# One transformer kernel, two edits: the last projection with tokens on partitions, and attention work issued in joined runs

## The chip, the cores and the metric

The kernel runs on one core of one Trainium2 chip. The metric is the device time of one execution in microseconds (us); lower is better. Three runs of the kernel before gave 1349.24, 1351.93 and 1356.86 us, median 1351.93. A profiled execution is one further run, with every instruction recorded.

## The reference

One sequence of 256 tokens with 1024 features passes through two blocks, all in float32. The first block has a modulated feed-forward net, a mixer that adds a short convolution and an attention of 8 query and 2 key heads, and a second feed-forward net. The second block has an even layer (gated recurrent heads and stick-breaking attention) and an odd layer (pooling). What the change touches:

```python
# first block: q and k are normed per head of 128 features, rotated, and attend
q = rms_norm(q.reshape(B, L, 8, 128), q_g);  k = rms_norm(k.reshape(B, L, 2, 128), k_g)
q = apply_axial_rope(q, cos, sin);           k = apply_axial_rope(k, cos, sin)
p = softmax(q @ k.T * 128 ** -0.5);          o = p @ v
# second block, mLSTM of the even layer: gates per head, broadcast over features
# second block, end of the odd layer, which is the kernel's output
y = (mixed * silu(z)) @ w_out            # 256 x 2048 @ 2048 x 1024
out = x + y * rsqrt(mean(y * y, axis=-1) + 1e-6) * post_g
```

## The kernel before

Activations lie with features on partitions and tokens along the free axis: `X[:, k, 256:512]` holds features 128k to 128k+127 of all 256 tokens. Each large product is made of three: weights and activations are split into a high and a low part in a rounded float32 format (`WH`, `WL`, `XH`, `XL` and so on), and TensorE adds high x high, high x low and low x high (lines 1038 to 1040; 1044 to 1046 where tokens are to lie on partitions, as for the values of the attention). Weights arrive in chunks of 4 x 128 rows by 256 columns: SyncE loads them (`W`), ScalarE makes the high part (`WH`, line 1458), VectorE the low part (`WL`, line 1863). A chunk is 24 products.

The order of all engines comes from one list, written by the class `Plan`. It walks through the large products; after each half chunk (12 products) it calls `tick`, which lets one of the background generators (`qk_norm`, `attention`, `mlstm`, ...) put its next step into the list. A `yield` in a generator is thus one half chunk of distance. Every engine then goes through the list and emits its own part of each step, so what is early in the list is early in the queue of every engine. Background steps take their PSUM tiles from banks 4 to 6 in turn (`bank`), the large products use banks 0 to 3, sums for norms bank 7 (`NB`).

Names that the change and the steps touch:
- `qk_norm`: the step `qs` squares a head on ScalarE, `qa` sums over its features by a matmul with 4 columns (`hot`, line 1125), `qb` broadcasts the reciprocal roots of a group of four heads from 4 rows to 128 partitions (line 1131), `rope` rotates by a matmul with `perm` (line 1136).
- `attention`: 16 rounds. `score` is one matmul of 512 columns (line 1142), a maximum and a scale on VectorE (lines 2045, 2047) and the exponential on ScalarE (line 1550). `scale` divides by the sum on VectorE (lines 2052, 2054), `turn` transposes four 128x128 blocks (line 1147) and ScalarE copies them out, `gather` multiplies by the values (line 1154), every second round.
- `m0` of `mlstm`: two broadcasts of gates from 4 rows (lines 1182, 1183), then the score products (lines 1189, 1191).
- evictions on VectorE in the mixer: `vc` (convolution, lines 1755 to 1764, eight small instructions a product), `bg`, `mc`.
- the end: products `p1` (four, of 16 x 128 rows and 256 columns), sums of squares by GpSimd and three matmuls with ones (`ones`, line 1000), the step `post` with the root on ScalarE (line 1525), the reciprocal (line 2010) and for each of eight feature tiles a multiply and an add on VectorE (lines 1718, 1724), and a DMA for each tile (line 979).
- GpSimd otherwise does nothing but the sums of squares (line 1256).

## Time and profile before

| what | value |
|---|---|
| median of three runs | 1351.93 us |
| profiled execution: its time, its span | 1357.65 us, 1355.9 us |
| mean granted TensorE clock | 0.989 of full speed |
| TensorE matmul busy | 1320.6 us, 97% |
| VectorE busy | 906.0 us, 67% |
| ScalarE busy | 648.1 us, 48% |
| GpSimd busy | 30.3 us, 2% |
| chain that ended last | TensorE 88%, VectorE 7%, ScalarE 3% |

The span runs from the first to the last instruction. Busy shares do not add up, since the engines work beside one another. The chain that ended last is followed back from the last instruction through whatever released each step. Matmuls are pipelined: one of 256 columns is recorded with about 0.28 us, but the next starts 0.11 to 0.12 us after it, so prices are read from starts. A matmul in full float32 appears as two records.

### The profile page before, as it was taken

What the parts mean: (1) busy time and instruction counts of PE and PEld (TensorE: products, weight loads), DVE (VectorE), ACT (ScalarE), POOL (GpSimd) and SP (SyncE); (2) the same over time, 40 slices, a digit from 0 to 9 for tenths busy, and PEclk for the clock granted to TensorE, in tenths of its full rate; (3) what the DMA queues carried; (4) which work ended last, traced back from release to release, by engine and by line L of the source; (5) the groups of instructions that cost most, each with busy time, mean ns of one, the idle gap of its engine ahead of it and who ended that gap; (6) DMA issues with size and microseconds to landing.
All of it is one profiled execution on the core that took longest, in us unless ns stands there. A gap on an engine that the chain in (4) does not pass through costs nothing.

```text
span 1355.9 us, 23439 instructions
## 1 busy us (share of the span) xinstructions
PE 1320.6 (97%) x9310; PEld 1212.0 (89%) x9310; DVE 906.0 (67%) x1462; ACT 648.1 (48%) x1025; POOL 30.3 (2%) x29
## 2 busy tenths in 40 slices
PE   6999999999999999999999999999999999999996
PEld 3688888888898889999999999998999999999996
DVE  3577875646658487654775555678886665689873
ACT  4433222223236335554454444566665765556552
POOL 0000000000010000000000000200000000100000
PEclk6999999999999999999999999999999999999998
DMA  8755656465544334444546655565546455437650
GB/s 303 262 166 188 206 193 218 161 216 184 176 153 156 109 113 152 127 150 148 183 142 186 199 175 172 155 188 157 169 135 193 126 166 177 140 119 215 196 172 32
DMA packets 201404, 229.69 MB, mean 169 GB/s; under 512 B 7120, under 2 KB 191696, under 8 KB 201296
## 3 DMA queue, kind: packets, MB, share of 16 engines
q1 hardware_dynamic: 201008, 227.90, 53.0%
q8 instruction: 75, 1.23, 0.4%
q14 instruction: 33, 0.27, 0.1%
q10 hardware_dynamic: 288, 0.29, 0.1%
HBM read 227.11 MB, written 1.05 MB: 168 GB/s over the span
## 4 chain that ended last, share of the span: by engine, by line
PE 88%; DVE 7%; ACT 3%; issue 2%; DMA 0%; DVEq 0%; ACTq 0%
PE P L1038 26%; PE P L1039 25%; PE P L1040 25%; DVE WL L1863 1%; PE P L1044 1%; PE P L1046 1%; PE P L1045 1%; PE P L1154 1%; DVE TS L1791 1%; PE P L1142 1%; PE P L1000 1%; PE P L1084 1%; DVE TS L1663 1%; ACT WH L1458 1%; PE P L1131 1%
## 5 line engine op out<-in xcount | busy, mean ns | idle before, releaser
L1038 PE MATMUL P<-XHB,WH 128*128 128x256 f32 (+1 forms) x1808 | 561.2, 310 | 7.5 <-DVE XLB L1675 3.7
L1039 PE MATMUL P<-XLB,WH 128*128 128x256 f32 (+1 forms) x1808 | 545.9, 302 | 0.0
L1040 PE MATMUL P<-XHB,WL 128*128 128x256 f32 (+1 forms) x1808 | 545.7, 302 | 0.0
L1863 DVE TENSOR_TENSOR WL<-W,WH 128x1024 fp32r<-128x1024 f32 x358 | 431.1, 1222 | 100.1 <-ACT WH L1458 99.9
L1458 ACT ACTIVATE WH<-W 128x1024 fp32r<-128x1024 f32 x358 | 368.7, 1041 | 251.4 <-PE P L1040 175.8
L1038 PEld LDWEIGHTS P<-XHB,WH 128*128 128x128 f32 x1808 | 341.9, 189 | 35.4 <-issue 14.0
L1039 PEld LDWEIGHTS P<-XLB,WH 128*128 128x128 f32 x1808 | 340.7, 188 | 18.0 <-issue 3.1
L1040 PEld LDWEIGHTS P<-XHB,WL 128*128 128x128 f32 x1808 | 340.6, 188 | 14.6
L1038 PE MATMUL P<-GH,WH 128*128 128x256 f32 (+1 forms) x372 | 122.0, 328 | 0.0
L1040 PE MATMUL P<-GH,WL 128*128 128x256 f32 (+1 forms) x372 | 121.5, 327 | 0.0
L1039 PE MATMUL P<-GL,WH 128*128 128x256 f32 (+1 forms) x372 | 121.5, 326 | 0.0
L1739 DVE TENSOR_TENSOR TS<-TS,P 128x512 f32<-128x512 f32 (+1 forms) x44 | 24.3, 554 | 83.0 <-PE P L1040 83.0
L1038 PEld LDWEIGHTS P<-GH,WH 128*128 128x128 f32 x372 | 70.7, 190 | 6.4 <-issue 0.2
L1039 PEld LDWEIGHTS P<-GL,WH 128*128 128x128 f32 x372 | 70.0, 188 | 6.4 <-issue 0.2
L1040 PEld LDWEIGHTS P<-GH,WL 128*128 128x128 f32 x372 | 70.0, 188 | 6.0
L1930 DVE CUSTOM_DVE_ANT_0 W<-W,AC,V 128x1024 f32<-128x1024 f32 x56 | 72.7, 1298 | 0.0
L1327 ACT ACTIVATE GH<-TS 128x512 fp32r<-128x512 f32 (+1 forms) x44 | 23.1, 526 | 92.3 <-DVE TS L1739 92.3
L1321 ACT ACTIVATE TS<-P 128x512 f32<-128x512 f32 (+1 forms) x44 | 21.4, 491 | 86.5 <-PE P L1040 86.5
L1256 POOL TENSOR_TENSOR SQ<-SQ 128x256 f32<-128x256 f32 (+1 forms) x25 | 30.1, 1205 | 1303.8 <-ACT SQ L1282 1302.7
L1749 DVE SCALAR_TENSOR_TENSOR X<-P,GM,X 128x256 f32<-128x256 f32 x48 | 21.5, 480 | 53.5 <-PE P L1040 53.4
L1044 PE MATMUL P<-WH,XHB 128*128 128x256 f32 x160 | 45.6, 285 | 1.1 <-DVE WL L1863 1.0
L1046 PE MATMUL P<-WH,XLB 128*128 128x256 f32 x160 | 44.5, 278 | 0.0
(302 smaller groups left out, 1813.8 us busy)
## 6 DMA issues: line engine op xcount, KB each, us to landing
W<-in_ffn_w_in SPq DMA_DIRECT2D x88, 512.0 KB, 4.8
W<-in_w_in_ab SPq DMA_DIRECT2D x72, 512.0 KB, 4.5
W<-in_w_modt SPq DMA_DIRECT2D x56, 512.0 KB, 3.9
W<-in_w_in SPq DMA_DIRECT2D x52, 512.0 KB, 3.6
W<-in_ffn_w_out SPq DMA_DIRECT2D x40, 512.0 KB, 4.6
W<-in_w_in_c SPq DMA_DIRECT2D x32, 512.0 KB, 4.3
W<-in_w_mod SPq DMA_DIRECT2D x16, 512.0 KB, 7.1
W<-in_w_out_ab SPq DMA_DIRECT2D x16, 512.0 KB, 4.4
```

The source lines that it names most:

```text
L1038: pe.matmul(o, h[:, k, c], xh[:, kk, a:b], start=kk == 0, stop=False)
L1039: pe.matmul(o, h[:, k, c], xl[:, kk, a:b], start=False, stop=False)
L1040: mm = pe.matmul(o, l[:, k, c], xh[:, kk, a:b], start=False, stop=kk == gm.nk - 1)
L1044: pe.matmul(o, xh[:, kk, c], h[:, k, :], start=kk == 0, stop=False)
L1046: mm = pe.matmul(o, xl[:, kk, c], h[:, k, :], start=False, stop=kk == gm.nk - 1)
L1256: pool.tensor_tensor(SQ[:, 0, 0:n], SQ[:, 0, 0:n], SQ[:, 1 + (k - 1) % 2, 0:n], ALU.add) \
L1327: act.activation(GH[m][:, f % 12, :], TS[:, f % NS, 0:n], ACT.Copy).then_inc(S[f"hh{m}"], 1)
L1458: act.activation(h, a, ACT.Copy).then_inc(S["wh"], 1)
L1739: dve.tensor_tensor(TS[:, f % NS, 0:n], TS[:, f % NS, 0:n], ps, ALU.mult).then_inc(S[f"hm{m}"], 1)
L1749: up = dve.scalar_tensor_tensor(X[:, k, ca:cb], ps[:, ca - a:cb - a], GM[:, m - 1, v, k:k + 1], X[:, k, ca:cb], ALU.mult, ALU.add)
L1863: dve.tensor_tensor(l, a, h.bitcast(F32), ALU.subtract).then_inc(S["wl"], 1)
L1930: td = dve.tensor_tensor_reduce(a if v == s.c - 1 else JK[:, :, :], a, (AC0, AC1)[v][:, :, :], 1.0, vec("bmod", 8 * g + k), ALU.mult, ALU. ...
```

## The change

It has two parts. The last projection `p1` gets its operands the other way round, so that tokens lie on partitions. Sums of squares then run along rows: ScalarE adds them up while it squares, one root per partition is taken from 128x1 numbers, the gain `pg` is loaded as a row for all partitions, the residual `X` is turned by 16 transposes behind the last product (step `xt`), and each half of the tokens is finished by two combines and two DMAs. In the attention, the score of the next round, the gather and the transpose come in one visit of the generator, the exponential becomes a step of its own behind them (`exp`), and the rotations of `qk_norm` share a visit with a broadcast. Along with that, the broadcasts of roots and gates and the head sums use all 128 rows and columns, the rest being zeros that GpSimd fills in (`HOT`, and two rows of tiles of `G`). The shape of `out_x` becomes tokens by features.

```diff
-        self.call(self.stats, "s7")
         for i in range(4):
-            self.gemm("p1", i, w["w_out_c_2"], 0, 16, 256 * i, (0, T), first=i == 0, norm=i == 3)
-        self.call(self.post, 1)
+            self.gemm("p1", i, w["w_out_c_2"], 0, 16, 256 * i, (0, T), turned=False, first=i == 0, norm=i == 3)
+        for i in range(4):
+            self.call(self.residual, i)
...
+    def residual(self, i):
+
+        self.step("xt", a=i, bank=4 + i, free=self.bank_free.get(4 + i, ("sr", self.roots["n", 5])))
...
             yield
         todo = None
         for i in range(4):
+            if todo is not None:
+                self.rope(*todo)
+                todo = None
             b, f = self.bank(self.up("qn"))
             self.step("qb", a=s, b=i, c=self.at("qn"), bank=b, free=f)
-            at = self.at("qn")
-            yield
-            if todo is not None:
-                self.rope(*todo)
-                yield
-                todo = None
             if s < 2 or i % 2:
-                todo = (s, i, at)
+                todo = (s, i, self.at("qn"))
             else:
                 self.ready.add(self.name(s, i))
-                self.end[self.name(s, i)] = at
+                self.end[self.name(s, i)] = self.at("qn")
+            yield
+            yield
         if todo is not None:
             self.rope(*todo)
 
...
         for _ in range(3):
             yield
         score(0)
+        self.step("exp", a=0, bank=4 + (self.uses - 1) % 3)
         for i in range(16):
-            yield
-            yield
+            for _ in range(2):
+                yield
             self.step("scale", a=i)
+            for _ in range(2):
+                yield
             if i + 1 < 16:
                 while missing(i + 1):
                     yield True
                 score(i + 1)
-            yield
+                bank = 4 + (self.uses - 1) % 3
             if i and i % 2 == 0:
                 b, f = self.bank(self.up("ol"))
                 self.step("gather", a=i // 2 - 1, bank=b, free=f)
-            yield
             b, f = self.bank(self.up("at"))
             self.step("turn", a=i, bank=b, free=f)
-        for _ in range(3):
+            if i + 1 < 16:
+                self.step("exp", a=i + 1, bank=bank)
+        for _ in range(2):
             yield
         b, f = self.bank(self.up("ol"))
         self.step("gather", a=7, bank=b, free=f)
...
+        HOT = MC[:, 0, 0:131]
-            G = sbuf(st, "G", [4, 6, T])
+            G = sbuf(st, "G", [128, 6, T])
-            return MC[0:4, 7, :] if s == 2 else RS[0:4, 1, T * s:T * s + T]
+            return MC[:, 7, :] if s == 2 else RS[:, 1, T * s:T * s + T]
...
+                if i == len(plan.loads) - 16:
+                    sp.wait_ge(S["k2p"], 8)
+                    sp.dma_start(PG, w["pg"].partition_broadcast(128).rearrange("p o c -> p (o c)")).then_inc(SI[5], 16)
...
-            for k in range(8):
-                sp.wait_ge(S["pst"], 8 + k + 1)
-                sp.dma_start(out[k * 128:k * 128 + 128, :], X[:, k, 256:512]).then_inc(S["out"], 16)
-            sp.wait_ge(S["out"], 16 * 8)
+            for n in range(4):
+                j, a = n // 2, n % 2
+                sp.wait_ge(S["p1o"], 4 * j + a + 3)
+                sp.dma_start(out[128 * j:128 * j + 128, 512 * a:512 * a + 512].rearrange("p (i c) -> p i c", i=2),
+                             X[:, 4 * j + 2 * a:4 * j + 2 * a + 2, 0:T]).then_inc(S["out"], 16)
+            sp.wait_ge(S["out"], 16 * 4)
...
-                    ones("s5" if s.a == 0 else "s7", 2)
-                    if s.a == 0:
-                        warm(3, s.b)
-                        pe.wait_ge(S["sr"], plan.roots["post", 0])
-                        warm(7, s.b)
+                    ones("s5", 2)
+                    warm(3, s.b)
+                    pe.wait_ge(S["sr"], plan.roots["post", 0])
+                    warm(7, s.b)
+                elif s.kind == "xt":
+                    pe.wait_ge(S["pst"], 8)
+                    for c in range(4):
+                        k = 4 * (s.a % 2) + c
+                        a = 256 + 128 * (s.a // 2)
+                        mm = pe.transpose(ps[:, c * 128:c * 128 + 128], X[:, k, a:a + 128], con("id"))
+                    mm.then_inc(S["xt"], 1)
                 elif s.kind == "qa":
+                    pe.wait_ge(S["fill"], 2)
                     for i in range(4):
                         n = 4 * s.a + i
                         pe.wait_ge(S["qs"], n + 1)
-                        pe.matmul(ps[0:4, 0:T], con("hot", 4 * i, 4 * i + 4), SQ[:, n % 3, T * (n // 3 % 2):T * (n // 3 % 2) + T], start=i == 0,
+                        pe.matmul(ps[:, 0:T], HOT[:, 3 - i:131 - i], SQ[:, n % 3, T * (n // 3 % 2):T * (n // 3 % 2) + T], start=i == 0,
                                   stop=i == 3).then_inc(S["qh"], 1)
                 elif s.kind == "qb":
                     pe.wait_ge(SI[5], 16)
                     if s.b == 0:
                         pe.wait_ge(S["qi"], s.a + 1)
-                    pe.matmul(ps[:, 0:T], con("sel", 128 * s.b, 128 * s.b + 128, 4),
+                    pe.matmul(ps[:, 0:T], con("sel", 128 * s.b, 128 * s.b + 128),
                               rows_of(s.a), start=True, stop=True).then_inc(S["qb"], 1)
...
-                    pe.matmul(ps[:, 0:T], con("sel", 128 * h, 128 * h + 128, 4), G[:, 4, 0:T], start=True, stop=True)
-                    pe.matmul(ps[:, T:2 * T], con("sel", 128 * h, 128 * h + 128, 4), G[:, 5, 0:T], start=True,
+                    pe.matmul(ps[:, 0:T], con("sel", 128 * h, 128 * h + 128), G[:, 4, 0:T], start=True, stop=True)
+                    pe.matmul(ps[:, T:2 * T], con("sel", 128 * h, 128 * h + 128), G[:, 5, 0:T], start=True,
...
+            pool.wait_ge(S["md"], 56)
+            pool.memset(HOT, 0.0).then_inc(S["fill"], 1)
+            pool.wait_ge(S["fill"], 1)
+            pool.memset(HOT[:, 3:4], 1.0).then_inc(S["fill"], 1)
...
+                if name == "s3":
+                    pool.wait_ge(S["oh"], 8)
+                    pool.memset(G[:, 4:6, :], 0.0).then_inc(S["fill"], 1)
...
-                        if kind == "p1":
-                            act.wait_ge(S["pst"], k + 1)
-                        act.activation(X[:, k, 0:T], ps, ACT.Copy, scale=vec("post" + kind[1], k)) \
-                            .then_inc(S[kind + "e"], 1)
+                            root_table(4)
+                        square("s5", k, (ps, 1.0))
+                        act.activation(X[:, k, 0:T], ps, ACT.Copy, scale=vec("post0", k)).then_inc(S["p0e"], 1)
+                    elif kind == "p1":
+                        if k == 4:
+                            root_table(5)
+                        if k >= 6:
+                            act.wait_ge(S["p1q"], k - 5)
+                        act.activation(SQ[:, k % 3, T * (k // 3 % 2):T * (k // 3 % 2) + T], ps, ACT.Square,
+                                       accum_out=FS[:, j, i:i + 1]).then_inc(S["p1q"], 1)
+                        if i == 3:
+                            act.wait_ge(S["p1o"], 4 * j + 1)
+                            act.activation(FS[:, j, 5:6], FS[:, j, 4:5], ACT.Sqrt, scale=1.0 / D, bias=con("eps")) \
+                                .then_inc(S["p1r"], 1)
...
-                elif s.kind == "score":
+                elif s.kind == "exp":
                     i = s.a
-                    act.wait_ge(S["am2"], i + 1)
+                    act.wait_ge(S["am1"], 2 * i + 2)
...
+            def root(j):
+
+                dve.tensor_reduce(FS[:, j, 4:5], FS[:, j, 0:4], AX, ALU.add).then_inc(S["p1o"], 1)
+                dve.wait_ge(S["p1r"], j + 1)
+                dve.reciprocal(FS[:, j, 6:7], FS[:, j, 5:6]).then_inc(S["p1o"], 1)
+                dve.wait_ge(S["p1o"], 4 * j + 2)
+                dve.wait_ge(S["p1e"], 6 + j + 1)
+                for a in range(2):
+                    y = X[:, 4 * j + 2 * a:4 * j + 2 * a + 2, 0:T]
+                    dve.wait_ge(S["xt"], 2 * j + a + 1)
+                    dve.scalar_tensor_tensor(y, y, FS[:, j, 6:7], P[:, 4 + 2 * j + a, :].rearrange("p (i c) -> p i c", i=2),
+                                             ALU.mult, ALU.add).then_inc(S["p1o"], 1)
...
+                        dve.wait_ge(S["p1q"], k + 1)
+                        dve.wait_ge(SI[5], 32)
+                        dve.tensor_tensor(X[:, 4 * j + i, 0:T], ps, PG[:, 256 * i:256 * i + 256], ALU.mult).then_inc(S["p1e"], 1)
+                        if i == 3:
+                            root(j)
...
-                    if s.a:
-                        for k in range(8):
-                            add(1, k)
...
-    out = nc.dram_tensor("out_x", (D, T), F32, kind="ExternalOutput").ap()
+    out = nc.dram_tensor("out_x", (T, D), F32, kind="ExternalOutput").ap()
     build_program(nc, aps, out)
     r = _run(nc, [{f"in_{n}": a for n, a in arrays.items()}], core_ids=[0])
-    return np.ascontiguousarray(r.results[0]["out_x"].T)[None]
+    return r.results[0]["out_x"][None]
```

The first place is TensorE's queue in the attention, in a round with a gather. `K,Q` is the score, `PT,VV` the gather, `C,TS` the transpose, `XHB,WH` and the like are large products. Before:

```order
L1040 MATMUL P<-XHB,WL 128x256
L1142 MATMUL P<-K,Q 128x512
L1038 MATMUL P<-XHB,WH 128x256
...
L1154 MATMUL P<-PT,VV 128x256 x4
L1038 MATMUL P<-XHB,WH 128x256
...
L1147 MATMUL P<-C,TS 128x128 x4
```

After:

```order
L1050 MATMUL P<-XHB,WL 128x256
L1159 MATMUL P<-K,Q 128x512
L1171 MATMUL P<-PT,VV 128x256 x4
L1164 MATMUL P<-C,TS 128x128 x4
L1048 MATMUL P<-XHB,WH 128x256
```

Three visits, 12 products apart, have become one. From a score to the transpose of the same round there are now 4 half chunks, before there were 6.

The second place is VectorE's queue in the same stage, from the maximum of a round (`TENSOR_REDUCE SM`) to its multiply (`TENSOR_SCALAR TS`), around the convolution of `vc3`. Before, the maximum comes behind the convolution or long ahead of it; in the round whose multiply waits for the convolution stands this:

```order
L1755 TENSOR_TENSOR U<-U,P 128x256
L1757 TENSOR_SCALAR TS<-U,V 128x256
L1760 SCALAR_TENSOR_TENSOR TS<-U,V,TS 128x256
L1764 SCALAR_TENSOR_TENSOR TS<-U,V,TS 128x256
L1863 TENSOR_TENSOR WL<-W,WH 128x1024
L2052 RECIPROCAL SM<-SM 128x1
L2054 TENSOR_SCALAR TS<-TS,SM 128x512
L2045 TENSOR_REDUCE SM<-P 128x1
L2047 TENSOR_SCALAR SM<-SM 128x1
```

After:

```order
L2090 TENSOR_REDUCE SM<-P 128x1
L2092 TENSOR_SCALAR SM<-SM 128x1
L1797 TENSOR_TENSOR U<-U,P 128x256
L1799 TENSOR_SCALAR TS<-U,V 128x256
L1802 SCALAR_TENSOR_TENSOR TS<-U,V,TS 128x256
L1806 SCALAR_TENSOR_TENSOR TS<-U,V,TS 128x256
...
L1911 TENSOR_TENSOR WL<-W,WH 128x1024
L2097 RECIPROCAL SM<-SM 128x1
L2099 TENSOR_SCALAR TS<-TS,SM 128x512
```

The maximum now stands directly ahead of the convolution (whose four instructions come twice), and the multiply of the same round behind it.

The third place is the end of VectorE's queue. Before, the last norm and the residual for each of eight tiles:

```order
L1718 TENSOR_TENSOR X<-X,RS 128x256
L1724 TENSOR_TENSOR X<-X 128x256
L1718 TENSOR_TENSOR X<-X,RS 128x256
L1724 TENSOR_TENSOR X<-X 128x256
```

After, from the last product with the gain of the first half of the tokens on:

```order
L1872 TENSOR_TENSOR X<-P,AC 128x256
L1757 TENSOR_REDUCE FS<-FS 128x1
L1759 RECIPROCAL FS<-FS 128x1
L1765 SCALAR_TENSOR_TENSOR X<-X,FS,P 128x2x256 x2
L1872 TENSOR_TENSOR X<-P,AC 128x256
L1757 TENSOR_REDUCE FS<-FS 128x1
L1759 RECIPROCAL FS<-FS 128x1
L1765 SCALAR_TENSOR_TENSOR X<-X,FS,P 128x2x256 x2
```

Sixteen instructions behind a reciprocal over 128x256 have become ten, with the combines of the first half ahead of the second half's gain.

## Rows read from the trace of the kernel before

**Rows 1.** The page: busy us and share of TensorE, records.

```profile
PE 1320.6 (97%) x9310; PEld 1212.0 (89%) x9310; DVE 906.0 (67%) x1462; ACT 648.1 (48%) x1025; POOL 30.3 (2%) x29
```

**Rows 2.** Waits of TensorE, one row: total us, times, longest us.

```profile
PE P L1147 <- DVE TS L2054: 0.5, 1, 0.5
```

**Rows 3.** Timeline of TensorE, a rotation: start us, duration us, instruction.

```profile
460.83 0.59 PE L1136 MATMUL P<-Q,C 128*128 128x256 f32 x2
...
461.38 0.28 PE L1039 MATMUL P<-XLB,WH 128*128 128x256 f32 x1
```

**Rows 4.** Timeline of TensorE, a broadcast of roots from 4 rows.

```profile
457.07 0.28 PE L1046 MATMUL P<-WH,XLB 128*128 128x256 f32 x1
457.28 0.69 PE L1131 MATMUL P<-RS,C 4*128 4x256 f32 x2
...
458.13 0.28 PE L1045 MATMUL P<-WL,XHB 128*128 128x256 f32 x1
```

**Rows 5.** Windows: stretch, length, busy us and records of each engine, clock, DMA.

```profile
699.00:880.00 181.00, 181.00 (x1538) 181.00 (x1538) 106.56 (x133) 92.19 (x132) 7.27 (x5) 1.00 0.59 181
...
1218.00:1341.00 123.00, 123.00 (x1085) 123.00 (x1086) 92.91 (x171) 68.83 (x113) 4.11 (x5) 1.00 0.53 163
```

**Rows 6.** Timeline of all engines, the tail behind the last product.

```profile
1343.50 0.28 PE L1040 MATMUL P<-RH,WL 128*128 128x256 f32 x1
...
1343.82 0.38 ACT L1282 ACTIVATE SQ<-P 128x256 f32<-128x256 f32 x1 [1.07 <-PE P L1040]
...
1345.49 1.75 DVE L2010 RECIPROCAL RS<-RS 128x256 f32<-128x256 f32 x1 [13.36 <-ACT RS L1525]
...
1353.30 0.43 DVE L1724 TENSOR_TENSOR X<-X 128x256 f32<-128x256 f32 x1
```

**Rows 7.** Timeline of TensorE, four transposes of the attention.

```profile
526.75 0.60 PE L1147 MATMUL P<-C,TS 128*128 128x128 f32 x4
...
527.30 0.28 PE L1039 MATMUL P<-XLB,WH 128*128 128x256 f32 x1
```

**Rows 8.** Groups by line: busy us, mean ns; the last, one line's durations.

```profile
L1739 DVE TENSOR_TENSOR TS<-TS,P 128x512 f32<-128x512 f32 x22 | 15.0, 687 | 54.7 <-PE P L1040 54.7
L2045 DVE TENSOR_REDUCE SM<-P 128x1 f32<-128x512 f32 x16 | 11.0, 687 | 4.9 <-PE P L1142 4.9
L2052 DVE RECIPROCAL SM<-SM 128x1 f32<-128x1 f32 x16 | 2.5, 156 | 0.0
L1288 ACT ACTIVATE SC<-C x5: 203/203/203, 389.7 to 1332.2; 128x1 f32<-128x1 f32 x5
```

**Rows 9.** DMA issues: count, KB each, median us from issue to landing.

```profile
W<-in_ffn_w_out SPq DMA_DIRECT2D x8, 256.0 KB, 4.3
out_x<-X SPq DMA_DIRECT2D x8, 128.0 KB, 1.7
```

**Rows 10.** Timeline of TensorE, a head sum with 4 columns, and four full matmuls.

```profile
475.80 1.89 PE L1125 MATMUL P<-SQ,C 128*4 128x256 f32 x8
...
477.85 0.28 PE L1039 MATMUL P<-XLB,WH 128*128 128x256 f32 x1
...
523.60 1.89 PE L1154 MATMUL P<-PT,VV 128*128 128x256 f32 x8
...
525.44 0.28 PE L1039 MATMUL P<-XLB,WH 128*128 128x256 f32 x1
```

**Rows 11.** Timeline of TensorE, the gates of one mLSTM head.

```profile
963.32 0.28 PE L1040 MATMUL P<-XHB,WL 128*128 128x256 f32 x1
...
966.12 0.28 PE L1045 MATMUL P<-WL,XHB 128*128 128x256 f32 x1
```

**Rows 12.** Timeline of VectorE, from a convolution's eviction to the multiply behind it.

```profile
544.21 0.42 DVE L1755 TENSOR_TENSOR U<-U,P 128x256 f32<-128x256 f32 x1 [1.26 <-PE P L1040]
...
549.08 0.49 DVE L2054 TENSOR_SCALAR TS<-TS,SM 128x512 f32<-128x512 f32 x1
```

**Rows 13.** One line of VectorE: durations, first and last start.

```profile
L1930 DVE CUSTOM_DVE_ANT_0 W<-W,AC,V x56: 1272/1279/2330, 72.2 to 368.8; 128x1024 f32<-128x1024 f32 x56
```

**Rows 14.** Timeline of GpSimd, the second sum of squares.

```profile
376.63 3.52 POOL L1256 TENSOR_TENSOR SQ<-SQ 128x512 f32<-128x512 f32 x2 [10.59 <-ACT SQ L1282]
```

More of the change, by code:

```diff
@@ L36 @@
 _at = 0
-for _name, _n in (("id", 128), ("one", 128), ("eps", 1), ("ee", 1), ("hot", 16), ("gat", 2), ("cnt", 26), ("perm", 128),
+for _name, _n in (("id", 128), ("one", 128), ("eps", 1), ("ee", 1), ("gat", 2), ("cnt", 26), ("perm", 128),
                   ("tri", 128), ("m01", 128), ("nst", 128), ("nca", 128), ("sel", 512), ("cos", 256), ("sin", 256)):
@@ L78, in constants @@
     put("ee", np.full((128, 1), EPS * EPS, np.float32))
-    hot = np.zeros((128, 4, 4), np.float32)
-    for i in range(4):
-        hot[:, i, i] = 1.0
-    put("hot", hot.reshape(128, 16))
     put("gat", (p[:, None] % 32 == np.arange(2)[None, :]).astype(np.float32))
@@ L846, in build_program @@
         seq, stat, end = plan.seq, plan.stat, plan.end
-        names = ("g wh wl zero sc mm mr mt mv md cb sf sq pa on sr ra ri rb am gm out sil1 hm1 hh1 hl1 xu1 sil2 hm2 hh2 hl2 xu2 "
+        names = ("g wh wl zero fill sc mm mr mt mv md cb sf sq pa on sr ra ri rb am gm out sil1 hm1 hh1 hl1 xu1 sil2 hm2 hh2 hl2 xu2 "
                  "nt nh nl xh xr rx "
                  "qe ke ve cge vce bge yh yl gte mce gae mae ma2 o2h o2l rse yc qs qh qr qi qb qn rm ro rd "
-                 "as am1 am2 ae an ap atp at agp oh ol two tw fr fin gr0 gmm gfree gab gq att cve cvs cvt cvq eve eoe "
-                 "ezt eze sqe ske sve szt sze m1 m1p m1t m2 m2p m3 m3p m4 m4p md1 md2 mhh m5 m5s m5p m5r m6 zh zl "
-                 "k1 k1p k1a k1l k1m k2 k2p k2e k3 k3p p0e p1e pst pm ope opc ph pl oze ome rh rl dv")
+                 "as am1 ae an ap atp at agp oh ol two tw fr fin gr0 gmm gfree gab gq att cve cvs cvt cvq eve eoe "
+                 "ezt eze sqe ske sve szt sze m1 m1p m1t m2 m2p m3 m3p m4 m4p md1 mhh m5 m5s m5p m5r m6 zh zl "
+                 "k1 k1p k1a k1l k1m k2 k2p k2e k3 k3p p0e p1e p1q p1r p1o xt pst pm ope opc ph pl oze ome rh rl dv")
         S = {n: ctx.enter_context(nc.semaphore(f"s_{n}")) for n in names.split()}
         SW = [ctx.enter_context(nc.semaphore(f"s_w{i}")) for i in range(WR)]
-        SI = [ctx.enter_context(nc.semaphore(f"s_in{i}")) for i in range(7)]
+        SI = [ctx.enter_context(nc.semaphore(f"s_in{i}")) for i in range(6)]
         def sbuf(st, name, shape, dt=F32):
@@ L877, in build_program @@
         RT = AM[:, 2, 1, 0:4]
+        FS = sbuf(ctx, "FS", [128, 2, 8])
         AC0 = sbuf(ctx, "AC0", [128, 4, 256])
@@ L2069, in _ @@
                     dve.wait_ge(S["gmm"], 1)
-                    dve.tensor_scalar(G[:, 1, 0:T], ps[0:4, T:2 * T], V[0:4, VEC["bf"][0]:VEC["bf"][1]], None, ALU.add) \
+                    dve.tensor_scalar(G[0:4, 1, 0:T], ps[0:4, T:2 * T], V[0:4, VEC["bf"][0]:VEC["bf"][1]], None, ALU.add) \
                         .then_inc(S["gfree"], 1)
                 elif s.kind == "g2":
-                    ig, b, t2, top, neg = (G[:, i, 0:T] for i in range(5))
+                    ig, b, t2, top, neg = (G[0:4, i, 0:T] for i in range(5))
                     dve.wait_ge(S["gfree"], 1)
@@ L2087, in _ @@
                     dve.wait_ge(S["dv"], own)
+                    dve.wait_ge(S["fill"], 3)
                     dve.tensor_scalar(neg, top, -1.0, None, ALU.mult).then_inc(S["dv"], 1)
```

59 lines of the change are left out of this document (28 added, 31 removed).

## The prediction

> **What bounds the kernel now.** I read the page first: TensorE is busy for 97% of the span [rows 1], on one core, and no other engine comes near it. The table of waits, limited to TensorE, then says how little it waits: in the stages that this change touches there is one entry that matters, a transpose of the attention that waited 0.5 us for VectorE [rows 2]. So time can come from three places only: from what TensorE issues, from the pace at which it issues, and from the tail behind the last product, where it has nothing left to do.
>
> *What it issues.* The timeline of TensorE shows an almost even stream of split products, one matmul of 256 columns each 0.11 to 0.12 us, broken by detours: small f32 matmuls for norms, attention and gates. The price of a detour is the time from the start of the product before it to the start of the second product behind it, less two ordinary steps. For a rotation by `perm` (128 rows, 256 columns) it is 461.38 - 460.83 - 0.12 = 0.43 us [rows 3]. For the broadcast of the roots, of the same 256 columns but with only 4 rows in the stationary and the moving operand, it is 458.13 - 457.07 - 0.24 = 0.82 us [rows 4]: the array stands for 0.1 us before it and for about 0.3 us behind it. Twelve such broadcasts are in the trace (24 records, two for an f32 matmul).
>
> *The pace.* The windows show that the even stream has two speeds although the granted clock is 1.00 (2.4 GHz) in all of them: 181.00 us / 1538 = 117.7 ns in the second feed-forward net, 123.00 / 1085 = 113.4 ns in the last stage [rows 5]. It changes only at a detour or a wait and then stays. Nothing in the diff aims at it, but it matters for the forecast below.
>
> *The tail.* From the start of the last product (1343.50) to the end of the span (1355.9) pass 12.4 us [rows 6]: the third sum by ones, the root over 128x256, a reciprocal of 1.75 us, eight times multiply and add on VectorE, and the last of eight DMAs.
>
> **The change, part by part.**
>
> *The tail.* Before, 3 matmuls with ones serve the last norm; the first of them stands inside the stream and costs a plain detour of 0.43 us, which goes. The new tail, from the start S of the last product:
> - TensorE turns the residual: 16 transposes, 4 to a bank. Four such transposes cost the attention 527.30 - 526.75 - 0.12 = 0.43 us [rows 7], so the first bank is ready at about S + 0.75 (the first answer to a product's end comes 0.32 us after its start, 1343.82 against 1343.50 [rows 6]), the second at S + 1.2, the last at S + 2.1.
> - The first half of the tokens is ahead: its last product ended 12 matmuls (1.4 us) earlier, so its square, sum, root and reciprocal are over by S + 0.7. VectorE's combine of 128x512 from PSUM is bounded by a 128x512 tensor op from PSUM, 0.69 us [rows 8]; with a scalar I take 0.70. Two of them end at S + 2.15.
> - Behind them on VectorE: the product with the gain for the second half (0.42), a sum over 4 numbers (0.16, as the reciprocal of 128x1 [rows 8]), on ScalarE a root of 128x1 (0.20 [rows 8]), the reciprocal (0.16), two combines (1.40), and four hand-overs of about 0.03: S + 4.6.
> - The last DMA. Now 2.17 us pass from the end of the last add (1353.30 + 0.43) to 1355.9, for 128 KB that landed in 1.7. The new piece is 256 KB. A 256 KB load took 4.3 us among others, 1.7 is for half the size [rows 9]. These are the two ends; the nearest row is the quiet 1.7, so I take 2.7 in all, at S + 7.3.
> The tail shrinks from 12.4 to 7.3, and with the detour the part is worth 5.1 + 0.4 = **5.5 us** (between 3.5 with a 4.3 us landing and 6.5).
>
> *The order of operands in the last product.* 384 products of 256 columns before and after; the values of the attention are made in the new order already, and such a product takes the same time. 0.
>
> *Full rows in the detours.* Twelve broadcasts go from 4 to 128 rows: 12 x (0.82 - 0.43) = **4.7 us**. Three column sums for q and k have 4 columns in the stationary operand: 477.85 - 475.80 - 0.12 = 1.93 plus 0.1 of entry = 2.03 us, where four full matmuls of the same width take 525.44 - 523.60 - 0.12 = 1.72 [rows 10]: 3 x 0.31 = **0.9 us**. The gates of the mLSTM begin with two 4-row broadcasts: 966.12 - 963.32 - 0.23 = 2.57 us for 1280 columns [rows 11], where full matmuls take 0.43 per 256, so 2.15; 3 x 0.42 = **1.3 us** (the first of the four heads keeps its 4-row transposes and so its switches). The other bound of all three is 0: the trace has no padded form of these very operations.
>
> The Trainium skill speaks on both sides here. "TensorE: Matmul & The Clock Gate", section "LDWEIGHTS (loading the stationary operand)", says that the row count does not matter, a 32-row load takes as long as a 128-row one; by that the padding would be worth nothing and the whole change 5.5 us. "TensorEngine Tiling", Key Properties, says that changing the tiling mode drains the engine; by that each 4-row detour pays twice, and padding removes it. The two detours of [rows 3, 4] differ by 0.39 us, so the trace sides with the second page.
>
> *The joined runs of the attention.* Score, gather and transpose stood apart, each between products; now they follow one another. A plain full-row detour costs no more than its own columns (0.43 for 256 [rows 3]), so joining saves at most some 0.01 us each, 0.3 in all. Against that, a score now has 4 half chunks (4 x 1.36 us) until its transpose, before 6. In series behind the score (512 columns, so 0.86 us) lie the maximum, 0.69 [rows 8], a scale, the copy of the previous transpose and the exponential on ScalarE over 512 columns each, a reciprocal and a multiply; six steps of at most 0.7 us with the score are about 4 us, which fits. But twice (`vc2`, `vc3`) VectorE must first evict a convolution: from its first instruction to the multiply pass 549.08 - 544.21 = 4.9 us, the queue that made the wait of [rows 2, 12]. Started after the maximum, 1.95 us behind the score's start, it ends at 6.85 + 0.49 = 7.3, and the transpose is due at 0.86 + 0.44 + 5.44 = 6.7: two waits of about 0.5 us. The old one (0.5, with its gap 0.67) goes. I book **0** (between -1 and +2).
>
> *Fills by GpSimd.* The first fill waits for the 56th modulation row (last at 368.8 [rows 13]) and stands ahead of the sums of squares. They need it only by 376.63, where the second sum began [rows 14]: about 6 us of slack. The load of the gain sits in SyncE's queue behind a wait for a sum that is over some 130 us earlier, and the queue runs ahead. 0; without that slack it would delay a norm by 1 to 2 us.
>
> Sum: 5.5 + 4.7 + 0.9 + 1.3 = 12.4 us. The profiled execution took 1357.65 (span 1355.9), so it would be 1345.3. It is the slowest of the four known times, 5.7 above the median of the runs, 1351.93; the slow pace in the second feed-forward net alone is 181 us x (1 - 113.4/117.7) = 6.6 us, about that distance, so I take the sum from the median: 1351.93 - 12.4 = **1339.5 us**. Its own range is 1334 to 1345.
>
> **Rivals.**
> 1. *The pace decides.* The runs lie at 1349 to 1357 with one program. A changed row of detours draws anew in which stretches the slow pace holds: one net more or less is 6.6 us, so 1333 or 1346. For it: the two paces and the spread. Against: a median of several runs evens it out.
> 2. *Full rows gain nothing*, because the 0.39 us comes from something else that a root broadcast does: 1339.5 + 6.9 = 1346.4. Against: three different operations show an excess, and the full-row forms between them do not.
> 3. *The attention becomes bound by its own chain (slower).* Place: the transposes, which wait for the multiply on VectorE. The price is what VectorE's queue adds per round; at 0.5 us in all 15 rounds the time is 1347. It decides from (12.4 + 6.8) / 15 = 1.3 us a round on, and with a whole eviction and a split in series in each round (2 us) the time is 1339.5 + 30 = 1369. For it: VectorE is the one engine with a full queue there. Against: only the convolution evictions are long, and they end with `vc3`.
> 4. *The new tail keeps its length*, the landing taking 4.3 us and the transposes coming late: 1339.5 + 3 = 1342.5.
>
> **How the numbers follow.** Forecast 0.66, rival 1 0.14 (half of it on each side), rival 2 0.06, rival 3 0.08 (0.04 mild at 1347, 0.04 slower), rival 4 0.06. Half a percent of 1351.93 is 6.8 us, about what a measurement of this kernel can tell from no change, so faster means below 1345.2 and slower above 1358.7. Faster: 0.66 x 0.96 + 0.07 + 0.06 = 0.76, and some of rivals 1 and 2 falls just below: 0.80. Slower: 0.04. The rest, 0.16, is same. Range: 1332 to 1348; it takes in rivals 1, 2, 4 and the mild form of 3.
>
> **What would show it.** The padded broadcasts in the timeline at 0.43 us by the count above; the sums at 1.72; the gates at 2.15. From the last product's start to the end 7 to 8 us; no reciprocal over 128x256 behind it. At most two or three waits of the transposes for VectorE, all below 1 us. Wrong would be: a gap ahead of and behind the padded forms as before, a table of waits in which the attention's transposes stand with 5 us or more, or a step of the stream that differs over whole stages from that of before.

## The result, and the profile after

| | before | after |
|---|---|---|
| median of 20 runs | 1357.17 us (1349.24 to 1363.64) | 1348.61 us (1347.10 to 1351.25) |
| ratio, 95% interval | | 0.9945, 0.9930 to 0.9961 |
| profiled execution: time, span | 1357.65, 1355.9 | 1351.25, 1349.3 |
| start of the last product to the end | 12.4 us | 7.3 us |

The change is faster by about 7.4 us, where 12.4 were forecast. The time itself, 1348.61, lies just outside the range of 1332 to 1348. The forecast started from 1351.93, the median of the first three runs of before; the median of all 20 is 5.2 us higher. These medians need one remark: its runs fall into two groups, 1349 to 1353 and 1355 to 1364, in shares that differ from one set of rounds to the next (5 of 20 here in the lower group, 30 of 31 in another set). The experiments show what such groups can come from. So a difference between two kernels is worth most where single stages are compared, and ratios carry their intervals.

I read the profile after by the steps of the prediction. The page first: TensorE has the span to itself as before [rows 1].

```profile
PE 1318.4 (98%) x9320; PEld 1219.2 (90%) x9320; DVE 903.8 (67%) x1461; ACT 645.1 (48%) x1026; POOL 27.0 (2%) x27
```

*The detours.* The timeline of TensorE (start, duration, instruction) at one broadcast of roots, which answers to [rows 4], then at one head sum, for [rows 10], and at the gates, for [rows 11]:

```profile
457.24 0.28 PE L1056 MATMUL P<-WH,XLB 128*128 128x256 f32 x1
457.36 0.59 PE L1148 MATMUL P<-RS,C 128*128 128x256 f32 x2
...
457.91 0.28 PE L1055 MATMUL P<-WL,XHB 128*128 128x256 f32 x1
...
474.21 0.28 PE L1050 MATMUL P<-XHB,WL 128*128 128x256 f32 x1
474.33 1.89 PE L1142 MATMUL P<-SQ,MC 128*128 128x256 f32 x8
...
476.17 0.28 PE L1049 MATMUL P<-XLB,WH 128*128 128x256 f32 x1
...
958.52 0.28 PE L1050 MATMUL P<-XHB,WL 128*128 128x256 f32 x1
...
960.93 0.28 PE L1055 MATMUL P<-WL,XHB 128*128 128x256 f32 x1
```

The broadcast costs 457.91 - 457.24 - 0.23 = 0.44 us, where 0.43 was forecast and 0.82 stood before; the gap ahead of it is gone (0.12 from the product before, a plain step). The sum costs 476.17 - 474.21 - 0.24 = 1.72 (forecast 1.72), the gates 960.93 - 958.52 - 0.23 = 2.18 (forecast 2.15). These three terms came out to a tenth of a microsecond.

*The tail.* The timeline of all engines behind the last product, for [rows 6]:

```profile
1341.99 0.28 PE L1056 MATMUL P<-WH,RL 128*128 128x256 f32 x1
...
1342.11 1.91 PE L1135 MATMUL P<-C,X 128*128 128x128 f32 x16
...
1342.85 1.41 DVE L1765 SCALAR_TENSOR_TENSOR X<-X,FS,P 128x512 f32<-128x512 f32 x2 [0.45 <-PE P L1135]
1343.62 3.39 SPq L988 DMA_DIRECT2D out_x<-X  x4
...
1345.21 1.41 DVE L1765 SCALAR_TENSOR_TENSOR X<-X,FS,P 128x512 f32<-128x512 f32 x2
```

The first combine starts 0.86 us behind the last product (its bank was forecast ready at 0.75), the last ends at 1345.21 + 1.41 = 1346.62, S + 4.63 (forecast 4.6), and 2.7 us pass from there to the end (forecast 2.7): 7.3 in all.

*The attention.* The table of waits of TensorE (total, times, longest) has no row for its transposes any more; the wait of [rows 2] has gone and the two that I expected did not come. The first rows:

```profile
PE P L1083 <- DVE SQ L1932: 7.3, 2, 4.4
PE P L1048 <- DVE XLB L1707: 3.7, 3, 1.4
PE P L1087 <- DVE TS L1939: 3.4, 1, 3.4
```

*Where the time is lost.* Detours and tail give what was forecast, and yet the last product starts at 1341.99 where it started at 1343.50: 1.5 us earlier, not 7.3. What is left is the pace of the stream, told below in ns a step, where a step is the time from the start of one product to the start of the next. The last projection, before and after:

```profile
1299.97 0.28 PE L1038 MATMUL P<-RH,WH 128*128 128x256 f32 x1
1300.09 0.28 PE L1039 MATMUL P<-RL,WH 128*128 128x256 f32 x1
1300.20 0.28 PE L1040 MATMUL P<-RH,WL 128*128 128x256 f32 x1
1300.31 0.28 PE L1038 MATMUL P<-RH,WH 128*128 128x256 f32 x1
```

```profile
1299.99 0.28 PE L1054 MATMUL P<-WH,RH 128*128 128x256 f32 x1
1300.11 0.28 PE L1055 MATMUL P<-WL,RH 128*128 128x256 f32 x1
1300.23 0.28 PE L1056 MATMUL P<-WH,RL 128*128 128x256 f32 x1
1300.35 0.28 PE L1054 MATMUL P<-WH,RH 128*128 128x256 f32 x1
```

Three steps took 0.34 us and take 0.36. By starts over long stretches the paces before were 113.3 and 117.8 ns a step; now there is a third, 120.0, at a granted clock of 1.00 as before. I took the starts of all groups of three products, stage by stage, and summed what they spend above 113.33 ns a step: 18.7 us in the trace before, 24.2 in the one after. The 5.5 us between them are what is missing: 5.1 (tail) + 0.4 + 6.7 (detours) + 0.8 (waits of the attention) - 5.5 = 7.5, and the spans differ by 6.6. Most of the 0.9 left lies in the first 40 us: the first matmul with `ROW` behind the first large products starts at 38.18 where it started at 37.39. The same products ran longer at the lower of the two clocks (1.2 GHz, a granted clock of 0.5) before TensorE was given 2.4 GHz. Over the stretch from 34 to 38 us the granted clock (third number from the end) was 0.89 before and 0.63 after:

```profile
34.00:38.00 4.00, 3.50 (x29) 2.21 (x27) 0.40 (x1) 0.38 (x1) 0.00 (x0) 0.89 0.11 23
```

```profile
34.00:38.00 4.00, 3.67 (x22) 1.84 (x20) 0.13 (x1) 0.26 (x1) 0.00 (x0) 0.63 0.00 0
```

A second trace of the changed kernel (`a_again` below) has 0.85 there, so this is no doing of the change.

The third pace holds in the products with `YH`, `OH`, `GH`, `ZH`, `PH` and `RH` alone. Those with `XHB` between them stay at 113.3 or 117.8. That asks for what such a tensor is to TensorE: a place in SBUF. The sizes of the tensors, taken to lie one behind the other in order of allocation, give the places. The change takes `hot`, 16 numbers or 64 bytes per partition, out of the constants `C`, which moves `X`, `W`, `WH`, `WL`, `XHB`, `XLB` and all up to `SC` down by 64 bytes. Behind `SC` it puts `FS`, 64 bytes, so that the operands of the stages stay where they were. From `WH` to `RH` there were 102080 bytes, 192 more than a multiple of 256; now there are 102144, a multiple of 256. The other stage operands of 256 columns stand in the same way. The allocations have gaps named `PAD2` to `PAD7`, which no instruction reads or writes, and `XHB` and `XLB` are a little longer than their data, so that two views of them can start at different places: all of it sets such distances.

### The profile page after: what moved, and what is told of

The parts are those of the page before. It is cut to its first block and busy times, and to the rows that moved or that the text cites. A ratio compares the mean times of both kernels' runs of the same rounds, so it can differ in the third digit from the quotient of the medians.

```text
span 1349.3 us, 23450 instructions
## 1 busy us (share of the span) xinstructions
PE 1318.4 (98%) x9320; PEld 1219.2 (90%) x9320; DVE 903.8 (67%) x1461; ACT 645.1 (48%) x1026; POOL 27.0 (2%) x27
## 5 line engine op out<-in xcount | busy, mean ns | idle before, releaser
L1048 PE MATMUL P<-XHB,WH 128*128 128x256 f32 (+1 forms) x1808 | 554.1, 306 | 7.2 <-DVE XLB L1707 3.7
L1054 PE MATMUL P<-WH,XHB 128*128 128x256 f32 x160 | 45.7, 285 | 1.3 <-DVE WL L1911 1.0
L1055 PE MATMUL P<-WL,XHB 128*128 128x256 f32 x160 | 44.7, 279 | 0.0
```

Source lines behind the costliest of these rows:

```text
L1048: pe.matmul(o, h[:, k, c], xh[:, kk, a:b], start=kk == 0, stop=False)
L1054: pe.matmul(o, xh[:, kk, c], h[:, k, :], start=kk == 0, stop=False)
L1055: pe.matmul(o, xh[:, kk, c], l[:, k, :], start=False, stop=False)
```

## Experiments

Medians and ratios are to the kernel before in the same rounds. The theories: A, the distance between weight tiles and stage operands sets the pace; B, the pace is drawn anew by any change in the row of detours; C, the turned product is slower.

**The places put back** (`a_place`, and once more as `a_place2`), on the changed kernel: a gap of 16 numbers where `hot` was, and `FS` allocated behind `PV`, as the last of all:

```diff
-... ("ee", 1), ("gat", 2), ...
+... ("ee", 1), ("gap", 16), ("gat", 2), ...
-        FS = sbuf(ctx, "FS", [128, 2, 8])
+            FS = sbuf(st, "FS", [128, 2, 8])
```

> The changed kernel with the places of before in SBUF: the 64 bytes of the table hot stay as a gap among the constants, and FS is allocated last. No instruction changes. Theory A (place): the pace of the large products hangs on where the operands of a stage (YH, OH, GH, ZH, PH, RH) lie against the weight tiles (WH, WL); the change moved the latter by 64 bytes and the former not. Then these products come back from 120.0 ns a step to 118 or less, and the time falls by about the 5.5 us that the forecast missed: 1343 us where the changed kernel has 1348.6, ratio to before 0.991. Theory B (draw): the pace is drawn anew by any change in the row of detours, whatever the places: the ratio stays 0.9945 within 0.001 and the stage products stay at 120.0 ns.

> a_place once more. Expected 1336 to 1337 us. If the choice between 113.4 and 117.8 ns is made anew in each execution, the last stage, at 117.8 in the first profile, or the second feed-forward net, at 113.4 there, can stand at the other pace, and the time goes with it; if it belongs to the program, all stages have the paces of the first profile.

Measured: 1336.56 us, ratio 0.9882 (0.9854 to 0.9910), and 1336.23, 0.9864 (0.9823 to 0.9904). The gain is larger than A had it, since the 5.5 us were read against a trace of before whose second net ran at 117.8 ns. B, which had the ratio at 0.9945 and the stage products at 120.0 ns, fell here and falls again with `b_shift`.

**The changed kernel again**, in the rounds of `a_place2`:

> The changed kernel once more, on the same chip and in the same rounds as a_place2. If the 64 bytes explain what the forecast missed, it stands at 1348 to 1349 us, about 12 us above a_place2, and its stage products are at 119 to 120 ns again (YH, OH, GH, ZH, PH, RH), without any at 113.4. If the paces are drawn anew in each execution, some of them are at 113.4 or 117.8 now.

Measured: 1348.93 us, 0.9948 (0.9923 to 0.9973), 12.7 us above `a_place2`. One row shows the pace of 381 steps in each: the third product with `RL`, 128 times, with first and last start (line, durations, starts). In the changed kernel, `a_again`, `a_place` and `a_place2`:

```profile
L1056 PE MATMUL P<-WH,RL x128: 283/283/284, 1296.3 to 1342.0; 128*128 128x256 f32 x128
```

```profile
L1056 PE MATMUL P<-WH,RL x128: 282/283/284, 1294.5 to 1340.2; 128*128 128x256 f32 x128
```

```profile
L1056 PE MATMUL P<-WH,RL x128: 278/280/282, 1288.2 to 1333.1; 128*128 128x256 f32 x128
```

```profile
L1056 PE MATMUL P<-WH,RL x128: 275/276/280, 1283.2 to 1326.3; 128*128 128x256 f32 x128
```

45.7 us in both executions of the changed kernel, 45.7 / 381 = 119.9 ns. With the places of before 44.9 us (117.8 ns) in one execution and 43.1 (113.1) in the other. So there is a draw, and it is made in each execution of one and the same program: the profiled run of `a_place` took 1342.84 us, its other five 1334.82 to 1337.12, and the profiled run of `a_place2` 1335.41. But between these two sets of places the draw is between 113.3 and 117.8 and was seen at the places of before alone; at the shifted ones the pace is 120.0 in both traces.

**The shift alone** (`b_shift`), on the kernel before:

```diff
         SC = sbuf(ctx, "SC", [128, 16])
+        sbuf(ctx, "PADX", [128, 16])
```

> The kernel before with 64 unused bytes behind SC, so that AC0 and all stage operands lie 64 bytes further from the weight tiles, the same distance as in the changed kernel; no instruction changes. Theory A: the products with PH, RH and ZH go from 113.4 to 119 to 120 ns, those with OH, YH and GH from 117.8 to 120 ns: about 8 us more, less what XHB gains (up to 3), so a ratio of 1.003 to 1.006. Theory B: ratio 1.000 and 113.4 ns in the last stage as before.

Measured: 1361.74 us, ratio 1.0067 (1.0042 to 1.0092), where A had 1.003 to 1.006. 64 bytes that nothing reads cost 9 us. Here the weight tiles kept their places and the operands moved, in the change it was the other way round; the paces are the same in both, so it is the distance that counts and not either place. Against the 15 of before's 24 runs that lie below 1352 (median 1350.3) the price is 11.5 us. The products with `RH`, here the moving operand, went to the third pace too: 46.2 us with a detour of 0.43, (46.2 - 0.43) / 381 = 120.1 ns.

```profile
L1041 PE MATMUL P<-RH,WL x128: 281/283/284, 1301.4 to 1347.6; 128*128 128x256 f32 x128
```

**One stage alone** (`a_pad7`), on `a_place`:

```diff
-            sbuf(st, "PAD7", [128, 64])
+            sbuf(st, "PAD7", [128, 80])
```

> a_place with 64 bytes more ahead of RH and PH alone (the gap of the last stage 320 bytes long, not 256); all other operands stay. Place theory: only the products with PH and RH go to 119 to 120 ns, 576 products of which the 384 with RH cost 2.2 to 6.6 ns each and the 192 with PH as much: 1.3 to 3.8 us more than a_place2, ratio 0.990 to 0.991; the stages before keep 113.4 or 117.8. Against it: another stage changes too, or this one doesn't.

Measured: 1339.97 us (1339.51 to 1340.43), 0.9875 (0.9833 to 0.9916), 3.7 above `a_place2`. The operands of the last stage alone went slow, the stages ahead kept paces seen at these places before (117.8 with `OH`, 113.3 with `GH`). The row as above, and for `OH`, which did not move, in `a_pad7` and then in the changed kernel (22.3 against 22.7 us for 189 steps):

```profile
L1050 PE MATMUL P<-OH,WL x64: 281/281/282, 634.7 to 657.0; 128*128 128x256 f32 x64
...
L1056 PE MATMUL P<-WH,RL x128: 283/283/286, 1285.3 to 1331.1; 128*128 128x256 f32 x128
```

```profile
L1050 PE MATMUL P<-OH,WL x64: 280/283/287, 638.0 to 660.7; 128*128 128x256 f32 x64
```

This trace also shows that the pace goes with the operands of the single product, and with nothing else that moved. In the last stage 24 products with `PH` and 48 or 144 with `XHB`, whose distance to the weights is that of before, follow one another without a detour between them. The first of such groups:

```profile
1213.13 0.28 PE L1048 MATMUL P<-PH,WH 128*128 128x256 f32 x1
...
1215.99 0.29 PE L1048 MATMUL P<-XHB,WH 128*128 128x256 f32 x1
...
1221.45 0.28 PE L1048 MATMUL P<-PH,WH 128*128 128x256 f32 x1
```

With `PH` a step takes (1215.99 - 1213.13) / 24 = 119.2 ns, with `XHB` right behind it (1221.45 - 1215.99) / 48 = 113.8 ns, and so it goes on up to the last projection; in the trace before both take 113.3. So it is the distance between the two operands of a matmul, and not a distance between other tensors, such as those that ScalarE and VectorE write meanwhile.

**Other distances** (`a_s32`, `a_s128`, `a_s192`): `a_place` with 8, 32 or 48 unused numbers behind `SC`, for distances of 224, 64 and 128 past a multiple of 256.

> a_place with 32 unused bytes behind SC, so the stage operands lie 224 bytes past a multiple of 256 from the weight tiles, where a_place has 192 and the changed kernel has 0. If only a distance of 0 is slow, this is as a_place: stage products at 113.4 or 117.8 ns, ratio 0.988 to 0.990. If 64-byte places matter (whole lines of the memory), 224 shares its line with 192, the same. If it grows with nearness, 119 ns and 0.991 to 0.994.

> a_place with 128 unused bytes behind SC: distance 64 past a multiple of 256. If only 0 is slow: as a_place, 113.4 or 117.8 ns in the products with OH, YH, GH, ZH, PH and RH, 0.988 to 0.990. If any place but the old one is slow: 120.0 ns as in the changed kernel, 0.994.

> a_place with 192 unused bytes behind SC: distance 128, as far from 0 as it goes. If only 0 is slow: 113.4 or 117.8 ns, 0.988 to 0.990. If the draw between 113.4 and 117.8 hangs on the distance too, this one shows a single pace in all stage products, 0.986 where it is 113.4.

Measured: 1347.97 us, 0.9974 (0.9962 to 0.9986); 1349.70, 0.9979 (0.9964 to 0.9993); 1348.73, 0.9981 (0.9969 to 0.9992). "Only 0 is slow" fell, and so did the other forecasts: all three lose most of the gain. Nor is it one slow pace for all other places. From the starts in the traces, ns a step:

| distance | kernel | `OH` | `GH`, second net | `ZH` | `PH` | `RH` |
|---|---|---|---|---|---|---|
| 192 | before | 117.8 | 117.8 | 113.5 | 113.3 | 113.4 |
| 192 | `a_place` | 117.8 | 113.4 | 113.4 | 117.8 | 117.8 |
| 192 | `a_place2` | 117.8 | 113.4 | 113.5 | 113.3 | 113.3 |
| 0 | after | 120.0 | 120.0 | 119.9 | 119.4 | 120.0 |
| 0 | `a_again` | 120.0 | 119.9 | 120.0 | 119.3 | 120.0 |
| 0 | `b_shift` | 120.0 | 119.9 | 120.0 | 119.1 | 120.0 |
| 224 | `a_s32` | 118.3 | 118.3 | 118.3 | 118.2 | 116.7 |
| 64 | `a_s128` | 117.8 | 117.8 | 113.7 | 117.8 | 113.4 |
| 128 | `a_s192` | 120.0 | 118.7 | 118.6 | 118.9 | 118.6 |

(`ZH` from the last 48 to 82 groups of its stage, where no detour stands between. In the traces of before, `a_place` and `a_place2`, 82 and 46 steps with `ZH` ahead of them ran at 117.8.) Each distance has paces of its own. Not all of the loss is theirs: in `a_s128` the products with `XHB`, whose distance did not change, spent 12.2 us above 113.3 ns a step, against 6.1 in `a_place2`, most of it because its second net drew 117.8; its runs lie in two groups too, three at 1345.4 to 1345.7 and seven at 1349.4 to 1350.8. `GH` of the first net, in products of 512 columns, adds to it: it stood at distance 0, and its pace there is 113.3 ns for 256 columns; a shift by 64 bytes makes it 114.5, by 32, 128 or 192 bytes 116.7. So the best distance is not even the same for all shapes, and I have no rule for it.

**Mixed distances** (`a_mix`): `a_place` with `PAD6` and `PAD7` of 96 numbers, distance 64 for the last two stages.

> a_place with 128 bytes more ahead of the operands of the last two stages (ZH, PH, RH), whose distance 64 gave 113.4 ns with RH and 114 with ZH in a_s128, but 117.8 with PH. If the pace belongs to the place: RH at 113.4, ZH at 114, PH at 117.8, so between 2 us faster than a_place2 and 1 us slower. If it was the draw: any mixture, the time within 3 us of a_place2.

Measured: 1338.66 us (1338.56 to 1346.19), 0.9879 (0.9833 to 0.9924). `RH` had 113.4 and `PH` 117.8 as in `a_s128`, but `ZH` 117.7 where that kernel had 113.7, so there is a draw at distance 64 as well. No gain over `a_place`.

**The parts of the change, one by one**, each on the kernel before with all places kept. `b_rows` has the full rows and their fills, `b_tail` the last projection and its tail, `b_join` the generators of the attention and of `qk_norm`; their diffs are the hunks of the change, each with the few semaphores that the change merged, which no run tests alone.

> The kernel before with nothing but the full rows: broadcasts of roots and gates and head sums over 128 rows and columns, with the fills by GpSimd; places in SBUF as before. The detours should cost 0.43, 1.72 and 2.15 us in place of 0.82, 2.03 and 2.57: 6.9 us less, ratio 0.995. Theory A expects the pace of before beside it (0.995 within 0.0015); theory B allows anything from 0.990 to 1.000 with another pattern of paces.

> The kernel before with nothing but the new last projection and its tail (FS allocated last, places as before). 5.5 us less by the tail and its detour, ratio 0.996, where the products of p1 keep 113.4 ns. Theory A says that they keep 113.4 or 117.8 ns, since the places are those of before; theory C (operands): the turned product itself is slower, 120.0 ns with RH in the stationary place, which costs 384 x 6.6 ns = 2.5 us and makes the ratio 0.998.

> The kernel before with nothing but the joined runs: score, gather and transposes of the attention in one visit, the exponential as a step of its own, a rotation beside a broadcast; places as before. Forecast: between -1 and +2 us, ratio 1.000, with two waits of the transposes of about 0.5 us. The chain theory (VectorE late in every round) gives waits of 0.5 us in 15 rounds, 1.005. The third theory (fewer breaks of the stream, so less to lose at each) gives up to 3 us less, 0.998, seen as a lower mean step between 500 and 633 us.

| kernel | median | ratio, interval | forecast |
|---|---|---|---|
| `b_rows` | 1345.36 | 0.9963, 0.9940 to 0.9986 | -6.9 us, 0.995 |
| `b_tail` | 1345.56 | 0.9948, 0.9926 to 0.9970 | -5.5 us, 0.996 |
| `b_join` | 1347.92 | 0.9976, 0.9963 to 0.9989 | 0 |
| product of the three | | 0.9887 | |
| `a_place` | 1336.56 | 0.9882, 0.9854 to 0.9910 | |
| after | 1348.61 | 0.9945, 0.9930 to 0.9961 | -12.4 us, 0.991 |

The parts multiply to what the change gives with its places kept. The lower groups alone say the same without the draw: in the rounds of `b_rows`, `b_tail` and `a_place` the lower group of before has a median of 1350.3 us, six of ten runs of `b_rows` have 1344.7 (5.6 us less) and seven of ten of `b_tail` 1345.0 (5.2 less); with the 3.1 between the medians of `b_join` and of before in its rounds that makes 13.9, where `a_place` is 13.7 below. Theory C fell with `b_tail`: the turned products ran at the same pace as the old ones.

```profile
L1056 PE MATMUL P<-WH,RL x128: 275/277/282, 1290.5 to 1333.7; 128*128 128x256 f32 x128
```

43.2 / 381 = 113.4 ns, with `RH` in the stationary place at distance 192.

`b_join` gives 3 us that I had booked at nothing. Two rounds of the attention, from a score to the one after the next, take 583.92 - 568.43 = 15.49 us before and 576.03 - 560.80 = 15.23 with the joined runs, with the same instructions in them. First before, then `b_join`:

```profile
568.43 1.02 PE L1142 MATMUL P<-K,Q 128*128 128x512 f32 x2
...
583.92 1.02 PE L1142 MATMUL P<-K,Q 128*128 128x512 f32 x2
```

```profile
560.80 1.02 PE L1145 MATMUL P<-K,Q 128*128 128x512 f32 x2
...
576.03 1.02 PE L1145 MATMUL P<-K,Q 128*128 128x512 f32 x2
```

That is 2.1 us in 8 pairs of rounds, and 0.8 us of waits go as well. The detours themselves cost the same, apart (0.86 + 0.86 + 1.73 + 2 x 0.44 = 4.33 in two rounds) or joined (1.30 + 3.03). The difference is the pace between them: the products with `XHB` in these rounds had 116.6 ns before and 116.8 in `b_rows`, but 113.6 in `b_join` and 113.7 in `a_place2`. This is the third theory of the expectation. It holds in 12 of the 14 traces: from the first score to the last the products with `XHB` had 115.8 to 116.8 ns in the four kernels with the detours apart (before, `b_rows`, `b_tail`, `b_shift`) and 113.5 to 113.8 in eight traces with joined runs. But `a_s32` and `a_s128` have joined runs too and had 116.6 and 117.4 there. So a detour can leave the stream in either pace, and joining them does not by itself fix which. Why the quicker one held is open.

## Why the prediction was wrong

*The step that failed* is the sentence on the pace: "Nothing in the diff aims at it." Nothing aims at it, but two lines of the diff set it, the removal of `hot` from the constants and the new tile `FS`. I had read both lines and costed them at nothing, as storage. The term that is missing is +12 us: `a_place2` against `a_again` gives 12.7 in the same rounds, `b_shift` against the lower group of before 11.5. Step by step: 525 products with `GH` in the second net x 6.5 ns = 3.4 us, 384 with `RH` x 6.7 = 2.6, 372 with `ZH` x 4.8 = 1.8, 192 with `PH` x 6.0 = 1.2, 192 with `OH` x 2.2 = 0.4, 369 with `YH` 1.5, and 936 steps of 256 columns with `GH` in the first net x 1.2 = 1.1: together 12.0.

*Rival 1* named the right quantity and the wrong cause. It had two paces, drawn anew, to either side. There are three, and the third is not drawn. It said that "a changed row of detours draws anew"; the runs show that the draw is made in each execution. This would explain the two groups of before (the second net at 117.8 ns costs 6.6 us, about the distance between them), but only one execution of before was traced, from the upper group, so that stays an estimate. They show too that the changed kernel, whose stage operands have one pace only, spreads over 4.2 us where before spreads over 14.4.

The prediction's reading of the paces was also too simple. "It changes only at a detour or a wait and then stays" does not hold in the trace that it was read from: at 909.14 the pace goes from 113.3 to 117.8 ns with no detour or wait, where products with tokens on partitions (line 1044) are followed by the others (line 1038).

*Tail*: right, in its length and in each of its steps. *Full rows*: right in the detours, 6.7 us by the traces; `b_rows` gives 5.6 us by the lower groups (2 to 8 by its interval), and no trace shows where the other 1.1 went. Rival 2 is refuted: the broadcasts went from 0.82 to 0.44. The Trainium skill ("TensorE: Matmul & The Clock Gate", section "LDWEIGHTS (loading the stationary operand)") says that a load of 32 rows takes as long as one of 128; that speaks of the load alone, and the prediction stretched it to the whole detour, which would have stayed at 0.82. The Trainium skill's other page, "TensorEngine Tiling", Key Properties, says that changing the tiling mode drains the engine, and the 0.38 us that went with the 4-row form agree with it. *Order of operands*: 0 as said, if the places are kept.

*Joined runs*: booked at 0, worth 3.2 us (1.5 to 5.0). Two things failed. The two waits did not come because the due time was wrong: the transposes stand behind the next score (0.86 us) and, from the third round on, one gather (1.73) always lies between a score and its transposes, so they were due at 0.86 + 0.44 + 5.44 + 0.86 = 7.6 us behind their score in the first two rounds and at 9.3 in the later ones, not at 6.7. VectorE's multiply ended at 542.79 + 0.49 = 543.28 in a round with a convolution, 7.2 us behind the score at 536.07, where the transposes came at 545.40:

```profile
541.06 0.48 DVE L1806 SCALAR_TENSOR_TENSOR TS<-U,V,TS 128x256 f32<-128x256 f32 x1
541.46 1.22 DVE L1911 TENSOR_TENSOR WL<-W,WH 128x1024 fp32r<-128x1024 f32 x1
542.60 0.15 DVE L2097 RECIPROCAL SM<-SM 128x1 f32<-128x1 f32 x1
542.79 0.49 DVE L2099 TENSOR_SCALAR TS<-TS,SM 128x512 f32<-128x512 f32 x1
```

It was nearest in the second round: multiply over at 521.31, transposes at 521.71, 7.6 behind their score. And the stream between the detours got quicker, which no term had. Rivals 3 and 4 did not come true.

*The fills*: free, as said. The first came at 370.72, and the sum of squares behind it began at 371.12, ahead of the second at 378.39.

The account closes so. Against the lower group of before (1350.3) `a_place2` (1336.2) gives 14.1 us, about the forecast (12.4) and the joined runs (3.1), less what the rows (1.3) and the tail (0.3) fell short. The places take 12.7 back, which leaves 1.4. In 15 of the 20 runs that the result is measured against, before stood in its upper group, 6.6 us higher: 0.75 x 6.6 = 5.0. The sum is 6.4 us, inside the measured 5.3 to 9.5 (0.9961 to 0.9930). So most of the measured gain is owed to how often before stood in its upper group, which was luck as far as the forecast goes.

## What to carry to other kernels

Where TensorE sets the time and its stream has no gaps, as here, the distance in SBUF between the two operands of a matmul is part of the kernel. A change that adds or drops a small tensor moves everything allocated behind it; read the diff for allocations first, and keep the places with a gap of the same size, here 64 bytes for 12 us. Before a structural change is judged, compare the steps of the stream by operand name in both traces: a pace that has changed in untouched products comes from the places or from the draw, not from the work that was restructured.

## What the runs showed of the hardware

- A stream of products of 256 columns at full granted clock runs at 113.3, 117.8 or 120.0 ns a step, and at values between with some distances. Starts are printed to 10 ns, so a single step read from them tells nothing; only long stretches do.
- At a distance of 192 bytes past a multiple of 256 a stretch of the stream has 113.3 or 117.8 ns, and two executions of one program can differ: the last stage had 117.8 in `a_place` and 113.3 in `a_place2`. Some stretches did not vary: `OH` had 117.8 in all eight traces at that distance.
- At one distance the pace changed at detours and waits, and also without one, where products of the one order of operands follow those of the other: 113.3 to 117.8 at 909.14 in the trace before. In all 14 traces the products behind that point ran at 117.7 or 117.8.
- A full f32 matmul of 256 columns with 4 rows costs the stream 0.82 us, one with 128 rows 0.43; with zeros in the other 124 rows the former costs 0.44.
- What joins distance and pace, no run here shows.
